# The two weight tiles of a block interleaved column by column in the weight buffers

## The chip, the cores and the metric

The kernel runs on one NeuronCore of a Trainium2 chip, as one launch. The metric is the device time in microseconds, the median of several executions. Three executions of the kernel before took 3079.48, 3080.9 and 3082.37 us. A fourth one was profiled, and all rows below come from that one.

## The reference

Two transformer-like blocks run one after the other on 256 tokens of width 2048, in float32. The first has a mixer (a gated delta rule and a gated convolution), cross attention on 256 memory tokens and a squared-ReLU MLP. The second has latent attention, neighbourhood attention, a Fourier mix and a gated convolutional feed-forward net, with a modulation worked out from one conditioning vector. What fills the time is the chain of dense products between them, of which these lines are typical:

```python
h = h + hybrid_mixer(rms_norm(h, norm_mix_g[i]), w_in[i], ...)          # x @ w_in, ... @ w_out
h = h + memory_cross_attention(rms_norm(h, norm_xa_g[i]), rms_norm(mem, norm_mem_g[i]), ...)
h = h + squared_relu_mlp(rms_norm(h, norm_mlp_g[i]), mlp_w1[i], mlp_w2[i])
...
x = x + gt1 * (jnp.concatenate([o_mla, o_na, o_fn], axis=-1) @ w_out[l])
x = x + gt2 * conv_ffn(h2, w_up[l], conv_w[l], conv_b[l], w_down[l])
```

## The kernel before

All dense weights are laid out on the host in one array `stream` of slots. A slot is 128 partitions x 1024 float32 columns, 512 KB, and there are 906 of them. A `Phase` is one dense product: `nblocks` blocks of `ncol` output features (256, in the two `kr` phases 128), each block made of `chunks` chunks of 128 input features. A slot holds `per_slot` chunks of one block (4; in `kr` 8), chunk after chunk, each `ncol` columns wide.

SyncE's queue loads the slots in order into a ring of eight buffers `raw`. ScalarE rounds each slot into one of four `whi` buffers (L823, fp32r, the reduced float32 that TensorE takes in one pass), and VectorE writes the remainder `raw - whi` into the matching `wlo` buffer (L1218). The activations are split in the same way into `act[:, 0]` and `act[:, 1]` (or `hid`). One product is then three matmuls: high weights with high activations, high with low, low with high.

TensorE's loop is `phase` (L448 is its matmul). For each block it waits for a free PSUM bank, for each slot for `split_done`, and then runs over the chunks of the slot, over the two halves `hf` of the block's 256 output features and over the three matmuls. In an ordinary phase the 128 x 128 weight tile is the stationary operand `lhs` and the 128 x 256 activations are the moving operand `rhs`; the two halves write the two halves of one PSUM bank. In a flipped phase (`memv`, `nav_c`, `nav_x`, `v_c`, `v_x`) the activations are the stationary operand and all 256 weight columns of the chunk the moving one. After the last matmul of a slot `slot_used` tells ScalarE that the `whi` and `wlo` buffers may be written again; it waits for nothing finer than a slot.

In the weight buffers of an ordinary phase a chunk's 256 columns stand in the order of the output features: first the 128 columns of half 0, then the 128 of half 1. Every weight tile is thus read with step one. The order of the work is written out: the phases follow each other in one fixed list, and each engine has its own copy of that order.

The modulation is worked out beside phases marked `mod`: VectorE accumulates `modacc` (L1204, L1423), and TensorE sums it in short matmuls with a one-column moving operand (L463, function `mod_matmuls`). Other short float32 matmuls are row sums (L469), a norm's spreading over partitions (L473), and those of the delta rule (L586 to L643). L586 and L588 take a stationary operand whose 128 columns are one column repeated.

Of the kernel before, what the change touches and what calls it, by code (L numbers as in the profile page):

```python
# [14 lines left out]
P = 128  # L15
# [112 lines left out]
def build(nc, x_t, mem_t, ctx_t, stream, mods, pvec, eye, cmix, catt, na_bias, na_mask, out_t):  # L128
    es = ExitStack()
    with es:  # L130
# [288 lines left out]
        def _(pe):  # L419
            c = Counts(pe)  # L420

            def phase(ph, src, c0=0, after=None):

                def body(i):
                    for k in range(ph.K):
                        b = bank[(ph.block0 + k) % 2]

                        pe.wait_ge(block_free, i * ph.K + (ph.block0 + k + 1))  # L430
                        for sl in range(ph.slots_per_block):
                            j = k * ph.slots_per_block + sl

                            pe.wait_ge(split_done, i * ph.S + (ph.slot0 + j + 1 + RAW_N))
                            if after and k == 0:
                                c.at(after[0], after[1] + (sl + 1) * after[2])
                            buf = (ph.slot0 + j) % SPL_N
                            for ci in range(ph.per_slot):
                                kc = sl * ph.per_slot + ci
                                for hf in range(ph.ncol // P if not ph.flip else TT):  # L440
                                    for n, (wx, ax) in enumerate(((whi, 0), (whi, 1), (wlo, 0))):
                                        if ph.flip:
                                            lhs = src[:, ax, c0 + kc, hf * P:(hf + 1) * P]
                                            rhs = wx[:, buf, ci * NCOL:(ci + 1) * NCOL]
                                        else:
                                            lhs = wx[:, buf, ci * ph.ncol + hf * P:ci * ph.ncol + (hf + 1) * P]
                                            rhs = src[:, ax, c0 + kc, :]
                                        mm = pe.matmul(b[:, hf * T:(hf + 1) * T], lhs, rhs,  # L448
                                                       start=(kc == 0 and hf == 0 and n == 0),
                                                       stop=(kc == ph.chunks - 1 and n == 2), skip_group_check=True)  # L450
                            mm.then_inc(slot_used, 1)
                            if ph.mod and j == MOD_OUT_AT:
                                mod_matmuls(ph, i)
                for i in range(ph.iters):
                    body(i)

            def mod_matmuls(ph, i):

                mb = i + ph.mod0
                pe.wait_ge(mod_used, mb * 8 + (8 + MOD_N))  # L460
                for w in range(ph.mod):
                    for n in range(MOD_COL // P):
                        mm = pe.matmul(bank[2][:, 4 * w + n:4 * w + n + 1], modacc[:, w, n * P:(n + 1) * P],  # L463
                                       ones[:, 0:1], start=True, stop=True, skip_group_check=True)
                mm.then_inc(mod_out, 1)
# [1267 lines left out]
def slots_of(w, ph, cols=None):  # L1733


    if cols is not None:
        w = np.concatenate([w[:, a:b] for a, b in cols], axis=1)
    n = ph.nblocks * ph.ncol
    assert w.shape == (ph.chunks * P, n), (ph.name, w.shape)
    w = w.reshape(ph.slots_per_block, ph.per_slot, P, ph.nblocks, ph.ncol)  # L1740
    return w.transpose(3, 0, 2, 1, 4).reshape(ph.slots, P, SLOT)


# [127 lines left out]
```

## Time and profile before

| what | value |
|---|---|
| median of three executions | 3080.9 us (3079.48 to 3082.37) |
| the profiled execution | 3077.71 us |
| its span, first to last instruction | 3075.9 us |
| what lies around the span | 1.8 us |
| mean granted TensorE clock | 0.970 |
| TensorE matmul / weight load busy | 2901.8 us / 2838.5 us |
| VectorE / ScalarE busy | 2096.0 us / 1331.7 us |
| weight slots loaded | 906 of 512 KB |

PE is TensorE's matmuls, PEld its weight loads, DVE VectorE, ACT ScalarE. A group is written out<-in; for L448 the two names behind the arrow are the moving and the stationary operand, so `bank<-act,whi` is an ordinary phase and `bank<-whi,act` a flipped one. Float32 operands that aren't fp32r show two records for each matmul. Busy matmul time is a modelled length and not a rate: matmuls overlap in the pipeline. The rate is read from the distance between starts, or from the number of records in a stretch.

### The profile page before, as it was taken

What the parts mean: (1) busy time and instruction counts of PE and PEld (TensorE: products, weight loads), DVE (VectorE), ACT (ScalarE), POOL (GpSimd) and SP (SyncE); (2) the same over time, 40 slices, a digit from 0 to 9 for tenths busy, and PEclk for the clock granted to TensorE, in tenths of its full rate; (3) what the DMA queues carried; (4) which work ended last, traced back from release to release, by engine and by line L of the source; (5) the groups of instructions that cost most, each with busy time, mean ns of one, the idle gap of its engine ahead of it and who ended that gap; (6) DMA issues with size and microseconds to landing.
All of it is one profiled execution on the core that took longest, in us unless ns stands there. A gap on an engine that the chain in (4) does not pass through costs nothing.

```text
span 3075.9 us, 55206 instructions
## 1 busy us (share of the span) xinstructions
PE 2901.8 (94%) x23858; PEld 2838.5 (92%) x23858; DVE 2096.0 (68%) x2934; ACT 1331.7 (43%) x1646; POOL 5.1 (0%) x13
## 2 busy tenths in 40 slices
PE   7998888999999899999999989988998999999998
PEld 7998787999998899999999979967598999999998
DVE  6988654698977877676766775454457665665665
ACT  4445323443433453444435444434345543554453
POOL 0000000000000000000000000000000000000000
PEclk9999898999999999999999989998999999999999
DMA  5554102577664677777777745522144565555553
GB/s 203 188 169 165 55 1 80 204 254 260 245 227 168 240 289 275 280 274 268 287 268 267 282 140 178 190 98 96 55 156 153 195 199 196 191 195 196 192 195 117
DMA packets 160451, 591.58 MB, mean 192 GB/s; under 512 B 17840, under 2 KB 17840, under 8 KB 159696
## 3 DMA queue, kind: packets, MB, share of 16 engines
q1 hardware_dynamic: 159264, 579.93, 53.4%
q0 software_dynamic: 944, 8.12, 0.7%
q8 instruction: 188, 3.08, 0.4%
q14 instruction: 55, 0.45, 0.1%
HBM read 585.88 MB, written 2.10 MB: 191 GB/s over the span
## 4 chain that ended last, share of the span: by engine, by line
PE 86%; DVE 10%; ACT 2%; issue 1%; DMA 1%; SPq 0%; DVEq 0%; ACTq 0%
PE bank L448 76%; DVE wlo L1218 2%; PE bank L712 1%; DVE ev L1237 1%; DVE modacc L1423 1%; PE bank L469 1%; PE bank L463 1%; PE bank L616 1%; PE bank L473 1%; DVE tmp L1373 1%; PE bank L614 1%; PE bank L608 1%; DVE ev L1340 1%; PE bank L687 1%; ACT whi L823 1%
## 5 line engine op out<-in xcount | busy, mean ns | idle before, releaser
L448 PE MATMUL bank<-act,whi 128*128 128x256 f32 x10144 | 1784.4, 281 | 59.7 <-DVE wlo L1218 20.2
L448 PEld LDWEIGHTS bank<-act,whi 128*128 128x128 f32 x10144 | 1560.0, 191 | 65.4 <-issue 34.1
L1218 DVE TENSOR_TENSOR wlo<-raw,whi 128x1024 fp32r<-128x1024 f32 x906 | 1098.1, 1223 | 530.2 <-ACT whi L823 528.4
L448 PE MATMUL bank<-act,wlo 128*128 128x256 f32 x5072 | 1421.7, 280 | 0.0
L823 ACT ACTIVATE whi<-raw 128x1024 fp32r<-128x1024 f32 x906 | 948.2, 1057 | 898.0 <-PE bank L448 897.4
L448 PEld LDWEIGHTS bank<-act,wlo 128*128 128x128 f32 x5072 | 969.4, 191 | 0.0
L448 PE MATMUL bank<-hid,whi 128*128 128x256 f32 x3456 | 602.5, 279 | 0.0
L448 PEld LDWEIGHTS bank<-hid,whi 128*128 128x128 f32 x3456 | 524.5, 188 | 0.0
L448 PE MATMUL bank<-hid,wlo 128*128 128x256 f32 x1728 | 482.1, 279 | 0.0
L1204 DVE SCALAR_TENSOR_TENSOR modacc<-modraw,small,modacc 128x512 f32<-128x512 f32 x480 | 348.6, 747 | 11.0 <-DMA modraw<-mods 5.6
L448 PEld LDWEIGHTS bank<-hid,wlo 128*128 128x128 f32 x1728 | 328.8, 190 | 0.0
L448 PE MATMUL bank<-whi,act 128*128 128x256 f32 x896 | 158.1, 279 | 0.0
L448 PEld LDWEIGHTS bank<-whi,act 128*128 128x128 f32 x896 | 136.5, 188 | 0.0
L448 PE MATMUL bank<-wlo,act 128*128 128x256 f32 x448 | 125.0, 279 | 0.0
L1293 DVE SCALAR_TENSOR_TENSOR ev<-bank,pv,ev 128x255 f32<-128x255 f32 x176 | 76.9, 478 | 62.8 <-ACT ev L888 61.3
L1423 DVE SCALAR_TENSOR_TENSOR modacc<-modraw,modacc 128x256 f32<-128x256 f32 x232 | 98.6, 481 | 0.1
L448 PEld LDWEIGHTS bank<-wlo,act 128*128 128x128 f32 x448 | 84.1, 188 | 0.0
L888 ACT ACTIVATE ev<-bank,pv 128x256 f32<-128x256 f32 x88 | 45.0, 561 | 70.4 <-PE bank L448 70.4
L901 ACT ACTIVATE ev<-h 128x512 f32<-128x512 f32 x40 | 25.3, 632 | 113.6 <-DVE h L1268 68.0
L1282 DVE TENSOR_TENSOR hid<-ev,hid 128x512 fp32r<-128x512 f32 x32 | 22.2, 693 | 72.8 <-ACT hid L877 72.8
L893 ACT ACTIVATE ev<-ev 128x256 f32<-128x256 f32 x44 | 18.4, 419 | 80.1 <-DVE ev L1293 80.1
L1014 ACT ACTIVATE tmp<-bank 128x512 f32<-128x512 f32 x28 | 16.7, 597 | 73.6 <-PE bank L608 73.6
(269 smaller groups left out, 1545.3 us busy)
## 6 DMA issues: line engine op xcount, KB each, us to landing
raw<-stream SPq DMA_DIRECT2D x906, 512.0 KB, 4.4
modraw<-mods SPq DMA_DIRECT2D x192, 512.0 KB, 4.1
h<-x_t SPq DMA_DIRECT2D x4, 512.0 KB, 6.3
memV<-mem_t POOLq DMA_DIRECT2D x1, 2048.0 KB, 8.6
tmp<-ctx_t POOLq DMA_DIRECT2D x1, 2048.0 KB, 12.5
out_t<-tmp SPq DMA_DIRECT2D x4, 512.0 KB, 2.6
cz<-catt POOLq DMA_DIRECT2D x1, 1216.0 KB, 12.2
bias<-na_bias POOLq DMA_DIRECT2D x1, 1024.0 KB, 5.1
```

The lines of the kernel that those rows point to most:

```text
L448: mm = pe.matmul(b[:, hf * T:(hf + 1) * T], lhs, rhs, start=(kc == 0 and hf == 0 and n == 0), stop=(kc == ph.chunks - 1 and n == 2), skip_ ...
L463: mm = pe.matmul(bank[2][:, 4 * w + n:4 * w + n + 1], modacc[:, w, n * P:(n + 1) * P], ones[:, 0:1], start=True, stop=True, skip_group_che ...
L469: return pe.matmul(out, src[:, tok], ones[:, 0:1], start=start, stop=stop, skip_group_check=True)
L473: return pe.matmul(out, small[:, col + n:col + n + 1].to_broadcast([P, P]), ident[:, :], start=start, stop=True, skip_group_check=True)
L608: mm = pe.matmul(bk(hg, 0)[:, n, :], MT[hg][:, n, :], X[hg][:, n, :], start=True, stop=True)
L614: pe.matmul(bk(hg, 2)[:, n, :], XT[hg][:, n, :], Y[hg][:, n, :], start=True, stop=True)
L823: sc.activation(whi[:, at % SPL_N, :], raw[:, at % RAW_N, :], ACT.Copy).then_inc(hi_done, 1)
L888: ins = sc.activation(ev[:, 0, hf * T:(hf + 1) * T], b2(b)[:, hf, :], ACT.Identity, scale=par("ff_conv", n * 6 + (6 * first + 3 * hf + 1)) ...
L1204: ins = ve.scalar_tensor_tensor(acc, wt, col, acc, ALU.mult, ALU.add)
L1218: ve.tensor_tensor(wlo[:, at % SPL_N, :], raw[:, at % RAW_N, :], whi[:, at % SPL_N, :].bitcast(F32), ALU.subtract).then_inc(split_done, 1)
L1293: ins = ve.scalar_tensor_tensor(o, b2(b)[:, hf, so], par("ff_conv", n * 6 + (6 * first + 3 * hf + j)), o, ALU.mult, ALU.add)
L1423: ins = ve.scalar_tensor_tensor(acc, x_, w, acc, ALU.mult, ALU.add)
```

## The change

The host lays the 256 columns of a chunk in another order, for ordinary phases only: column 0 of half 0, column 0 of half 1, column 1 of half 0, column 1 of half 1, and so on. The kernel's `lhs` for half `hf` is then every second column, starting at column `hf`: a stationary operand of 128 columns with a step of two elements (8 bytes) where it had one of a step of one (4 bytes). The splits on ScalarE and VectorE work on whole slots, whatever the order of their columns. Flipped phases keep their layout and operands. In the `kr` phases, where a block has 128 columns, the expression gives the same operand as before. No buffer moves, and no instruction, wait or transfer is added or taken away.

```diff
@@ phase, TensorE
                                         else:
-                                            lhs = wx[:, buf, ci * ph.ncol + hf * P:ci * ph.ncol + (hf + 1) * P]
+                                            cols = wx[:, buf, ci * ph.ncol:(ci + 1) * ph.ncol]
+                                            lhs = cols.rearrange("p (n a) -> p a n", a=ph.ncol // P)[:, hf, :]
                                             rhs = src[:, ax, c0 + kc, :]
@@ slots_of, on the host
     w = w.reshape(ph.slots_per_block, ph.per_slot, P, ph.nblocks, ph.ncol)
+    if not ph.flip:
+        w = w.reshape(w.shape[:-1] + (ph.ncol // P, P)).swapaxes(-1, -2).reshape(w.shape)
     return w.transpose(3, 0, 2, 1, 4).reshape(ph.slots, P, SLOT)
```

## Rows read from the trace of the kernel before

**Rows 1.** The page: span, busy time and share of each engine, instructions

```profile
span 3075.9 us, 55206 instructions
PE 2901.8 (94%) x23858; PEld 2838.5 (92%) x23858; DVE 2096.0 (68%) x2934; ACT 1331.7 (43%) x1646; POOL 5.1 (0%) x13
```

**Rows 2.** The page: chain that ended last, share of the span by engine

```profile
PE 86%; DVE 10%; ACT 2%; issue 1%; DMA 1%; SPq 0%; DVEq 0%; ACTq 0%
```

**Rows 3.** Windows: stretch, busy and records of each engine, clock, DMA share, GB/s

```profile
1300.00:1500.00 200.00, 200.00 (x1702) 200.00 (x1701) 140.89 (x162) 90.02 (x97) 0.00 (x0) 1.00 0.75 277
...
2400.00:2600.00 200.00, 200.00 (x1767) 200.00 (x1766) 126.94 (x170) 93.24 (x109) 0.00 (x0) 1.00 0.58 193
```

**Rows 4.** The page: groups, busy us, mean ns, idle before and its releaser

```profile
L448 PE MATMUL bank<-act,whi 128*128 128x256 f32 x10144 | 1784.4, 281 | 59.7 <-DVE wlo L1218 20.2
...
L1218 DVE TENSOR_TENSOR wlo<-raw,whi 128x1024 fp32r<-128x1024 f32 x906 | 1098.1, 1223 | 530.2 <-ACT whi L823 528.4
L448 PE MATMUL bank<-act,wlo 128*128 128x256 f32 x5072 | 1421.7, 280 | 0.0
L823 ACT ACTIVATE whi<-raw 128x1024 fp32r<-128x1024 f32 x906 | 948.2, 1057 | 898.0 <-PE bank L448 897.4
...
L448 PE MATMUL bank<-hid,whi 128*128 128x256 f32 x3456 | 602.5, 279 | 0.0
...
L448 PE MATMUL bank<-hid,wlo 128*128 128x256 f32 x1728 | 482.1, 279 | 0.0
...
L448 PE MATMUL bank<-whi,act 128*128 128x256 f32 x896 | 158.1, 279 | 0.0
...
L448 PE MATMUL bank<-wlo,act 128*128 128x256 f32 x448 | 125.0, 279 | 0.0
```

**Rows 5.** Waits: who waited for whom, us in total, times, longest

```profile
ACT whi L823 <- PE bank L448: 897.4, 568, 8.5
...
DVE wlo L1218 <- ACT whi L823: 528.4, 433, 6.9
```

**Rows 6.** Timeline, weight loads at 2500 us: start us, us, instruction, count

```profile
2499.97 0.19 PEld L448 LDWEIGHTS bank<-act,wlo 128*128 128x128 f32 x1
...
2500.99 0.19 PEld L448 LDWEIGHTS bank<-act,wlo 128*128 128x128 f32 x1
```

**Rows 7.** Timeline, weight loads at 1500 us

```profile
1500.03 0.19 PEld L448 LDWEIGHTS bank<-act,wlo 128*128 128x128 f32 x1
...
1501.09 0.19 PEld L448 LDWEIGHTS bank<-act,wlo 128*128 128x128 f32 x1
```

**Rows 8.** Chain in order of time: start us, us, what, count

```profile
655.31 45.33 PE bank L448 x384
...
1735.70 45.34 PE bank L448 x384
...
2341.11 719.92 PE bank L448 x6336
```

**Rows 9.** Timeline, weight loads of L463 (one moving column) and after them

```profile
653.36 1.87 PEld L463 LDWEIGHTS bank<-ones,modacc 128*128 128x128 f32 x16
655.14 0.30 PEld L448 LDWEIGHTS bank<-act,whi 128*128 128x128 f32 x2
```

**Rows 10.** Timeline, weight loads of the delta rule at 424 to 429 us

```profile
424.54 0.47 PEld L591 LDWEIGHTS bank<-ident,qkvT 128*128 128x128 f32 x4
...
425.41 0.97 PEld L586 LDWEIGHTS bank<-cz,gt 128*128 128x128 f32 x8
...
428.07 0.97 PEld L598 LDWEIGHTS bank<-tmp,qkvT 128*128 128x128 f32 x8
```

**Rows 11.** Timeline of weight loads from 490 us

```profile
490.54 6.51 PEld L469 LDWEIGHTS bank<-ones,tmp 128*128 128x128 f32 x32 [2.02 <-ACT tmp L1031]
```

**Rows 12.** Window inside that stretch, columns as in rows 3

```profile
491.00:495.00 4.00, 4.00 (x21) 4.00 (x20) 0.00 (x0) 1.72 (x2) 0.00 (x0) 0.50 0.00 0
```

## The prediction before the run

> **What bounds the kernel now.** I read the page first: of a span of 3075.9 us TensorE's matmuls are busy for 94% and its weight loads for 92%, VectorE for 68% and ScalarE for 43% [rows 1]. The chain that ended last runs over PE for 86% [rows 2]. The windows say why a busy share isn't enough here: in 200 us inside the MLP and in 200 us inside the feed-forward net both matmuls and loads are busy all the time at full clock, and yet the first holds 1701 loads and the second 1766 [rows 3]. So the thing to read is the pace, the distance from one weight load to the next.
>
> The waits show which way the work leans. ScalarE's split waits 897.4 us for TensorE to give a buffer back, and VectorE's split waits 528.4 us for ScalarE [rows 5]; TensorE waits for VectorE's split for only 20.2 us in its largest group [rows 4]. TensorE is the bound, and everything else of the weight path is cover.
>
> Now the pace itself. At 2500 us nine loads take 2500.99 - 2499.97 = 1.02 us, 113.3 ns each [rows 6]. At 1500 us nine take 1501.09 - 1500.03 = 1.06 us, 117.8 ns each [rows 7]. Both are the same instructions with the same shapes, at a granted clock of 1.00 [rows 3]. The chain in order of time shows that each pace holds for long: nineteen pieces of 384 matmuls at 45.33 or 45.34 us (118 ns) between 655 and 1781 us, and 6336 in 719.92 us (113.6 ns) at the end [rows 8]. I call them the long and the short pace.
>
> What sets them? The moving operand is 256 columns; if it takes one column in each cycle of 2.4 GHz, that is an estimated 106.7 ns. The weight load can be seen nearly alone where the moving operand has one column: sixteen loads from 653.36 to 655.14 us, 111.3 ns each [rows 9]. By that estimate load and matmul are almost equally long. At half the clock 32 such loads take 6.51 us, or (6.51 - 0.33)/31 = 199 ns each if the last one lasts 0.33 us [rows 11, 12]: the pace goes with TensorE's clock, so it isn't a fixed time for issue. A load of the main loop has at most 113.3 - 111.3 = 2 ns of cover at the short pace and 6.5 ns at the long one. That is why this change can matter at all.
>
> **The change part by part.** *Host layout.* No device time. *Transfers and splits.* The slots are as large as before, and L823 and L1218 read and write them whole; their 1057 and 1223 ns [rows 4] stay. If they did not, they have the waits of rows 5 as cover. *Flipped phases*, 896 + 448 matmuls [rows 4]: untouched. *The two `kr` phases*, one block of 16 chunks and 3 matmuls each, 96 in all: same operand. *Ordinary phases*: 10144 + 5072 + 3456 + 1728 - 96 = 20304 loads [rows 4] read their 128 columns over 1024 bytes of each partition instead of 512. This is the only term: 20304 x d, where d is what a load's step adds to the pace. 1 ns of d is 20.3 us, 0.66% of the time. Nothing is re-ordered, so no wait and no queue moves; `slot_used` still comes after both halves of a slot.
>
> No load in the trace has a step of two, so d has to be bounded.
>
> *From below.* The nearest rows are loads at the other end, with all 128 columns taken from one address. L586 in rows 10 has eight such loads in 0.97 us, (0.97 - 0.19)/7 = 111 ns each; L598, eight loads of adjacent columns, gives the same 0.97 us. How many bytes the columns are spread over doesn't show there, from 4 to 512. The transposes of L591 give (0.47 - 0.14)/3 = 110 ns, though each of their loads is recorded at about 0.14 us instead of 0.19 [rows 10, 6]: so float32 columns can be fetched faster than the main loop's loads fetch them, by some 50 ns in 128 columns, and what holds an ordinary load to 107 to 111 ns is then probably not the reading of adjacent bytes. That speaks for d = 0. A gain isn't excluded: the short pace is 113.3 against 110 to 111 in rows 9 and 10, and if the two streams of reads hinder each other, another order of addresses may free them. The bound is 2.3 ns for the short-paced loads and 6.5 ns for the long-paced ones.
>
> *From above.* If a load's 107 ns were set by the bytes that it passes over, twice the bytes would take 213 ns, and with the 4.6 ns that lie between 106.7 and 111.3 the pace would be 218 ns: d = 104.7 and 100.2 ns at the two paces, about 102.6 ns on average.
>
> I take d = 0, since one address against 512 bytes made no difference, and keep both ends.
>
> The Trainium skill has a rule that speaks against the change: "SBUF — State Buffer", section "Door 1: The DMA port swizzle", says that SBUF is read in lines of 16 bytes, that each crossing to a new line costs, and that at least two hits in a line are needed to hide this. Step two in float32 crosses twice as often, 64 lines a load and not 32, but has exactly two hits in each; so by the letter of the rule d is still 0, on its very edge. No row here has a step between one address and the next line, so the trace neither confirms nor denies it.
>
> The sum: 3077.7 us of the profiled execution (3075.9 of span and 1.8 around it) + 20304 x 0 = 3077.7 us. The median of the three runs lies 3.2 us higher, so on that scale it is 3080.9 us.
>
> **The rivals.**
>
> *The paces change hands, faster.* The long pace isn't a matter of addresses in the source: the same loop has both. Of the 21744 matmuls of L448 the nineteen pieces hold 7296, and with the shorter pieces beside them I estimate 10,000 long-paced ones and 11,000 short-paced ones. The first long-paced piece of rows 8 begins right behind the one-column matmuls of rows 9; my guess is that load stream and matmul stream can lock in two ways, and that such a break picks one. A load that reads other addresses may tip the lock. All at the short pace: 10,000 x 4.5 ns = 45 us less, 3036 us. Against it: three runs within 2.9 us say that the locks fall in the same way each time, and equal load times should leave them so.
>
> *The paces change hands, slower.* The same, with the short pace lost: 11,000 x 4.5 = 49.5 us more, 3130 us. Both streams would now walk at the same speed, 1024 bytes in 107 ns, where they walked at two different ones; a conflict, once there, would last for the whole matmul.
>
> *A price for each new line.* The mechanism of this kernel: 32 more lines in each of 20304 loads, with 2 ns of cover. With one cycle for each (0.417 ns at 2.4 GHz) a load grows by 13.3 ns; less the 2 or 6.5 ns of cover, some 9 ns remain, 180 us more, 3264 us. It decides where the short-paced loads alone grow by 6 us/10,300 = 0.6 ns past their cover, at (2 + 0.6)/32 = 0.08 ns a line. Where the skill's SBUF page says "each access that crosses to a new line pays a penalty", this is what it would be.
>
> *The load is bound by bytes passed over.* d = 102.6 ns: 20304 x 102.6 = 2083 us more, 5164 us. For it: a load is at the limit now. Against it: rows 10. Nothing else would become late; ScalarE and VectorE would only wait longer for TensorE.
>
> **How the numbers follow.** No change of pace: 0.60, with a range of its own of 3075 to 3087 us. Locks to the short pace: 0.10. A freer load that passes even the short pace (down to 111 ns everywhere, 3080.9 - 45 - 49 = 2987 us): 0.02. Locks to the long pace: 0.10. A price for each line: 0.10. Bound by bytes: 0.08. To leave out no more than 2 in 10 the range reaches over both lock rivals, 3034 to 3135 us: 0.60 + 0.10 + 0.10 = 0.80. Within 0.2% (6 us, about what a measurement of this kernel can tell from no change) 0.60, faster 0.12, slower 0.28.
>
> **What the profile after would show.** Right: 1701 and 1766 loads in the windows of rows 3, a pace of 113.3 and 117.8 ns at the places of rows 6 and 7, and the same waits as rows 5. Lock: the same two paces, but pieces of 384 in 43.5 us, or of 6336 in 746. A price for a line: one new pace over 118 ns in ordinary phases, with flipped phases still at 113 to 118, and the wait of L823 for TensorE grown by about as much as the span. Bytes: PEld records longer than 0.19 us and a pace near 218 ns. The prediction is wrong if the load's fetch has no spare rate at step two, which only the transposes' shorter load lets me hope for.

## The result, and the profile after

The change makes the kernel slower: 3160.18 us (3158.47 to 3161.47, four runs) against 3080.19 us (3073.06 to 3082.37, four runs) on the same chip, a ratio of 1.0263 with a 95% interval of 1.0246 to 1.0281. The time lies above the stated range, which ended at 3135 us.

The page after. TensorE is still the bound; both its shares rise a little, and the instructions are the same in number. The line numbers behind L448 have moved by one.

```profile
span 3156.7 us, 55206 instructions
PE 2990.5 (95%) x23858; PEld 2927.9 (93%) x23858; DVE 2102.5 (67%) x2934; ACT 1332.4 (42%) x1646; POOL 5.1 (0%) x13
PE 87%; DVE 9%; ACT 2%; issue 1%; DMA 1%; SPq 0%; DVEq 0%; ACTq 0%
L449 PE MATMUL bank<-act,whi 128*128 128x256 f32 x10144 | 1854.2, 284 | 53.6 <-DVE act L1368 14.4
L1219 DVE TENSOR_TENSOR wlo<-raw,whi 128x1024 fp32r<-128x1024 f32 x906 | 1101.8, 1222 | 586.8 <-ACT whi L824 580.4
L824 ACT ACTIVATE whi<-raw 128x1024 fp32r<-128x1024 f32 x906 | 948.9, 1057 | 965.8 <-PE bank L449 963.5
```

The splits cost what they did [rows 4], 1057 and 1222 ns. ScalarE waits 963.5 us for TensorE instead of 897.4 [rows 5], 66 us more while the span grew by 81: it stands farther behind the bound, as it would behind a TensorE that has become slower by itself.

The same two windows as in rows 3, and the weight loads at the place of rows 6, of the changed kernel:

```profile
1300.00:1500.00 200.00, 200.00 (x1671) 200.00 (x1670) 138.18 (x158) 88.27 (x96) 0.00 (x0) 1.00 0.73 271
2400.00:2600.00 200.00, 200.00 (x1669) 200.00 (x1668) 127.77 (x179) 91.48 (x114) 0.00 (x0) 1.00 0.58 187
```

```profile
2499.87 0.19 PEld L449 LDWEIGHTS bank<-act,wlo 128*128 128x128 f32 x1
...
2500.95 0.19 PEld L449 LDWEIGHTS bank<-act,wlo 128*128 128x128 f32 x1
```

Before, the two windows held 1701 and 1766 loads; now they hold 1670 and 1668. Nine loads take 2500.95 - 2499.87 = 1.08 us, 120.0 ns each. The two paces of 113.3 and 117.8 ns have become one in the ordinary phases, above both. The chain in order of time shows where that leaves the microseconds; each piece has its counterpart in rows 8:

```profile
1105.29 46.20 PE bank L449 x384
...
2378.95 762.49 PE bank L449 x6336
```

The last stretch of 6336 matmuls went from 719.92 to 762.49 us, 42.6 us of the 80.8 us by which the span grew. The nineteen pieces of 384 went from 45.34 to 46.20 us; one of them, in the flipped phase `memv`, stayed at 45.34, so the other 18 give 15.5 us. The rest is spread over the other pieces. Over 20304 changed loads the growth is 4.0 ns each.

### The profile page after: what moved, and what is told of

Its sections match the earlier page's. It is cut to its first block, busy times and chain, and to the rows that moved or that the text cites. A ratio compares the mean times of both kernels' runs of the same rounds, so it can differ in the third digit from the quotient of the medians.

```text
span 3156.7 us, 55206 instructions
## 1 busy us (share of the span) xinstructions
PE 2990.5 (95%) x23858; PEld 2927.9 (93%) x23858; DVE 2102.5 (67%) x2934; ACT 1332.4 (42%) x1646; POOL 5.1 (0%) x13
## 4 chain that ended last, share of the span: by engine, by line
PE 87%; DVE 9%; ACT 2%; issue 1%; DMA 1%; SPq 0%; DVEq 0%; ACTq 0%
PE bank L449 77%; DVE wlo L1219 2%; PE bank L713 1%; DVE ev L1238 1%; DVE modacc L1424 1%; PE bank L470 1%; PE bank L464 1%; PE bank L617 1%; DVE tmp L1374 1%; PE bank L474 1%; PE bank L615 1%; PE bank L609 1%; DVE ev L1341 1%; PE bank L688 1%; ACT whi L824 1%
## 5 line engine op out<-in xcount | busy, mean ns | idle before, releaser
L449 PE MATMUL bank<-act,whi 128*128 128x256 f32 x10144 | 1854.2, 284 | 53.6 <-DVE act L1368 14.4
L449 PEld LDWEIGHTS bank<-act,whi 128*128 128x128 f32 x10144 | 1616.4, 196 | 58.6 <-issue 33.4
L1219 DVE TENSOR_TENSOR wlo<-raw,whi 128x1024 fp32r<-128x1024 f32 x906 | 1101.8, 1222 | 586.8 <-ACT whi L824 580.4
L449 PE MATMUL bank<-act,wlo 128*128 128x256 f32 x5072 | 1442.6, 284 | 0.0
L824 ACT ACTIVATE whi<-raw 128x1024 fp32r<-128x1024 f32 x906 | 948.9, 1057 | 965.8 <-PE bank L449 963.5
L449 PEld LDWEIGHTS bank<-act,wlo 128*128 128x128 f32 x5072 | 993.7, 196 | 0.0
L449 PE MATMUL bank<-hid,whi 128*128 128x256 f32 x3456 | 623.5, 282 | 0.0
L449 PEld LDWEIGHTS bank<-hid,whi 128*128 128x128 f32 x3456 | 545.1, 194 | 0.0
L449 PE MATMUL bank<-hid,wlo 128*128 128x256 f32 x1728 | 488.5, 283 | 0.0
L609 PE MATMUL bank<-tmp 128*128 128x128 f32 x224 | 33.4, 299 | 15.5 <-DVE tmp L1526 8.6
```

The lines of the kernel that those rows point to most:

```text
L449: mm = pe.matmul(b[:, hf * T:(hf + 1) * T], lhs, rhs, start=(kc == 0 and hf == 0 and n == 0), stop=(kc == ph.chunks - 1 and n == 2), skip_ ...
L609: mm = pe.matmul(bk(hg, 0)[:, n, :], MT[hg][:, n, :], X[hg][:, n, :], start=True, stop=True)
L824: sc.activation(whi[:, at % SPL_N, :], raw[:, at % RAW_N, :], ACT.Copy).then_inc(hi_done, 1)
L1219: ve.tensor_tensor(wlo[:, at % SPL_N, :], raw[:, at % RAW_N, :], whi[:, at % SPL_N, :].bitcast(F32), ALU.subtract).then_inc(split_done, 1)
```

## The experiments

The question is why a weight load that takes every second column lengthens the pace by 2 to 7 ns. I name the candidates by what a load of 128 columns touches: with step one 512 bytes, 32 lines of 16 bytes; with step two 1024 bytes, 64 lines. The kernels from step four to the one with a moving step of two were run once each, so no interval stands beside their times; the readings rest on the distances between their loads.

**Step four**, an interleave of four tiles instead of two, with the host layout to match:

```diff
-                                            lhs = wx[:, buf, ci * ph.ncol + hf * P:ci * ph.ncol + (hf + 1) * P]
+                                            if ph.ncol == NCOL:
+                                                tile, a = ci * 2 + hf, 4
+                                                cols = wx[:, buf, tile // a * a * P:(tile // a + 1) * a * P]
+                                                lhs = cols.rearrange("p (n a) -> p a n", a=a)[:, tile % a, :]
...
+        w = w.reshape(ph.slots, P, 8 // 4, 4, P).swapaxes(-1, -2).reshape(ph.slots, P, SLOT)
```

> Four weight tiles (two chunks, two halves) interleaved, so that each weight load of an ordinary phase has a step of four elements, 16 bytes; the result is the same. After the change the pace of ordinary phases was 120.0 ns a matmul at full clock, against 113.3 or 117.7 before. Theory 1 (a price for each 16-byte line that a load enters): a load enters 128 lines where it entered 64, and with one hit in each. The growth from 32 to 64 lines was 6.7 ns against the shorter pace, so 64 more lines cost at least 13.4 ns more: a pace of 133 ns or above, near 3430 us. Theory 2 (the extra comes from the step not being one, whatever its size): 120 ns again, 3160 us. Theory 3 (load and moving operand collide when they walk through their bytes at the same speed, 1024 bytes in the length of one matmul): at step four they walk at different speeds again, so the pace falls back below 120 ns.

It took 5449.23 us. The loads of this kernel in the timeline:

```profile
2466.53 0.33 PEld L453 LDWEIGHTS bank<-act,wlo 128*128 128x128 f32 x1
...
2470.03 0.33 PEld L453 LDWEIGHTS bank<-act,wlo 128*128 128x128 f32 x1
```

Fifteen loads in 3.50 us, 233.3 ns each. The pace nearly doubled with the step. Theory 2 (any step but one costs the same) and theory 3 (the two streams collide only when they walk equally fast) fall; theory 1 had the direction, but where it asked for at least 13.4 ns more, 113 ns were added. The same kernel a little earlier, with its window:

```profile
2456.03 0.33 PEld L453 LDWEIGHTS bank<-act,wlo 128*128 128x128 f32 x1
...
2458.83 0.33 PEld L453 LDWEIGHTS bank<-act,wlo 128*128 128x128 f32 x1
```

```profile
2456.00:2459.00 3.00, 3.00 (x14) 3.00 (x14) 2.25 (x3) 0.00 (x0) 0.00 (x0) 0.50 0.15 42
```

Here the granted clock was 0.50 (1.2 GHz), and twelve loads took 2.80 us, again 233.3 ns. This length doesn't go with TensorE's clock, unlike that of a load with adjacent columns [rows 11, 12].

**Step zero**, all columns of a load from one address (the other columns are left out):

```diff
-                                            lhs = wx[:, buf, ci * ph.ncol + hf * P:ci * ph.ncol + (hf + 1) * P]
+                                            at = ci * ph.ncol + hf * P
+                                            lhs = wx[:, buf, at:at + 1].to_broadcast([P, P])
```

> The kernel before, but in ordinary phases all 128 columns of a weight load are the first column of the tile, repeated (step zero), so that a load stays in one 16-byte line; this leaves out the other columns, the products are other numbers. Theory 1 (price for each line): 31 lines fewer than before take away up to 6.5 ns, and the pace falls to the moving operand's own, 107 to 111 ns; near 2960 us. Theory 2 (adjacent bytes are the fast path, anything else pays): 120 ns, 3160 us. Theory 3 (collision of the two streams): something other than 113.3 and 117.7, most likely 107 to 111 ns.

It took 3068.28 us, against a single run of 3074.59 us of the kernel before on that chip. Its windows, pieces of its chain, and loads from the first of these pieces:

```profile
1300.00:1500.00 200.00, 200.00 (x1718) 200.00 (x1717) 141.93 (x164) 90.12 (x98) 0.00 (x0) 1.00 0.75 272
2400.00:2600.00 200.00, 200.00 (x1767) 200.00 (x1766) 126.40 (x167) 90.83 (x105) 0.00 (x0) 1.00 0.59 195
```

```profile
1083.69 46.19 PE bank L449 x384
1130.66 43.64 PE bank L449 x384
1175.09 44.91 PE bank L449 x384
...
2331.49 720.12 PE bank L449 x6336
```

```profile
1083.88 0.31 PEld L449 LDWEIGHTS bank<-act,whi 128*128 128x128 f32 x2
...
1085.56 0.19 PEld L449 LDWEIGHTS bank<-act,wlo 128*128 128x128 f32 x1
```

Loads from one line gained next to nothing, so the expectation of 2960 us was wrong, and so was a price that simply adds up by the line. The run doesn't give the length of such a load, though: the moving operand was as before, and it turns out below that this operand holds the pace. The pieces show more. Beside one-line loads the same matmuls ran at 43.64 us/384 = 113.6 ns, at 44.91/384 = 117.0 ns and at 46.19/384 = 120.3 ns; in the last of these fourteen loads take 1085.56 - 1083.88 = 1.68 us, 120.0 ns each. That is the pace of the changed kernel, without a step of two.

**Half of the moving columns**, with step one and with step two (the products of the other tokens are left out in 94 of 96 matmuls of a block):

```diff
+                                        w_ = T if (kc == 0 and n == 0) or ph.flip else T // 2
+                                        rhs = rhs[:, 0:w_]
-                                        mm = pe.matmul(b[:, hf * T:(hf + 1) * T], lhs, rhs,
+                                        mm = pe.matmul(b[:, hf * T:hf * T + w_], lhs, rhs,
```

> The kernel before, but in ordinary phases only 128 of the 256 moving columns are streamed in 94 of 96 matmuls of a block; this leaves out half of the tokens' products. Weight loads are unchanged, with step one. It shows the load without a full-length matmul over it. Load is what sets the pace: 111 to 113 ns a matmul stays, near 3030 us. Load and matmul only bind together: the pace falls clearly below 107 ns, as far as the load's own length.

> The changed kernel with the same cut to 128 moving columns. Theory 1 (lines) and any theory by which the step-two load is itself longer: the pace stays at 120 ns, some 7 to 9 ns above the same cut with step one. Theory 3 (collision with the moving operand): with the moving operand busy for half of the time the extra is halved or gone, so both cuts lie within 3 ns of each other.

They took 4887.06 and 4896.52 us: with half as many moving columns in each matmul the mean granted clock fell to 0.621 and 0.622, and the expected 3030 us was missed for that reason. Both hold the same 470 loads in a window at clock 0.50, 213 ns each, but they differ in a stretch of such matmuls at 1.00, which both have right behind a flipped phase, whose matmuls keep their 256 columns. First the kernel with step one, then that with step two:

```profile
3150.00:3190.00 40.00, 40.00 (x360) 40.00 (x360) 18.15 (x15) 17.81 (x19) 0.00 (x0) 1.00 0.58 195
2500.00:2600.00 100.00, 100.00 (x471) 100.00 (x470) 39.60 (x45) 21.82 (x22) 0.00 (x0) 0.50 0.45 158
```

```profile
3150.00:3190.00 40.00, 40.00 (x342) 40.00 (x342) 17.58 (x15) 16.77 (x18) 0.00 (x0) 1.00 0.55 184
2500.00:2600.00 100.00, 100.00 (x471) 100.00 (x470) 38.93 (x44) 21.82 (x22) 0.00 (x0) 0.50 0.45 158
```

40 us / 360 = 111.1 ns and 40 us / 342 = 117.0 ns. The load sets the pace even beside a matmul of half the length, and step two lengthens it by 6 ns there. At half the clock step two is free: the pace of 213 ns is longer than the 117 ns that the load with step two took in the other window.

**Step three and step eight.** The first reads every third column from a stretch of 384 (columns of other tiles; the products are other numbers), the second interleaves all eight tiles of a slot.

```diff
+                                                at = (ci + hf) * P
+                                                cols = wx[:, buf, at:at + 3 * P]
+                                                lhs = cols.rearrange("p (n a) -> p a n", a=3)[:, 0, :]
```

```diff
+                                                tile, a = ci * 2 + hf, 8
```

> The kernel before with a step of three elements (12 bytes) in the weight loads of ordinary phases; it reads columns that belong to other tiles of the same slot, so the products are other numbers. So far: step two, 64 lines of 16 bytes a load, 120.0 ns; step four, 128 lines, 233 to 236 ns. Theory A (each line that a load enters takes a fixed time, 120/64 = 1.88 or 235/128 = 1.84 ns, and the load takes the longer of that and its own length): 96 lines, 176 to 180 ns a matmul, near 4270 us. Theory B (two hits in a line hide it, fewer don't, as the rule of the lines reads by its letter): a third of the lines has two hits and the others one; a threshold would put the load near 235 ns, as step four, near 5450 us.

> All eight weight tiles of a slot interleaved: a step of eight elements, 32 bytes, same result. A load then enters 128 lines, as at step four, but passes over 4096 bytes instead of 2048. Theory A (lines entered): 233 to 236 ns as at step four, 5449 us within some 3%. Theory C (bytes passed over, which fits steps two and four as well: 120 and 235 ns for 1024 and 2048 bytes): about 470 ns, near 10,000 us.

Step three took 4211.54 us, step eight 5576.63 us. Their loads in the timeline:

```profile
2409.76 0.26 PEld L453 LDWEIGHTS bank<-hid,wlo 128*128 128x128 f32 x1
...
2411.84 0.26 PEld L453 LDWEIGHTS bank<-hid,wlo 128*128 128x128 f32 x1
```

```profile
1999.69 0.34 PEld L453 LDWEIGHTS bank<-hid,wlo 128*128 128x128 f32 x1
...
2001.86 0.34 PEld L453 LDWEIGHTS bank<-hid,wlo 128*128 128x128 f32 x1
```

Twelve loads in 2.08 us are 173.3 ns, nine in 2.17 us are 241 ns. By bytes passed over (theory C) step eight would have doubled step four; it is within 4% of it, so bytes are out and lines remain. The 4% between two loads of 128 lines each is not explained. By a threshold of two hits (theory B) step three would have been like step four; it lies at 96 lines x 1.81 ns.

**The moving operand.** Its 256 columns are 64 lines too. Two kernels repeat one moving column (the other tokens are left out), with loads of step one and of step two; a third gives the moving operand a step of two across a pair of chunks (other products), with loads of step one.

```diff
-                                            rhs = src[:, ax, c0 + kc, :]
+                                            rhs = src[:, ax, c0 + kc, 0:1].to_broadcast([P, T])
```

```diff
-                                            rhs = src[:, ax, c0 + kc, :]
+                                            pair = src[:, ax, c0 + kc - kc % 2:c0 + kc - kc % 2 + 2, :]
+                                            rhs = pair.rearrange("p k (t a) -> p (k t) a", a=2)[:, :, kc % 2]
```

> The kernel before, but in ordinary phases the 256 moving columns are all the chunk's first column, repeated, so that the moving operand stays in one 16-byte line where it entered 64; this leaves out all other tokens. Loads have step one. Theory M (the moving operand's lines are under the same limit of 1.8 to 1.9 ns each: 64 x 1.77 = 113.3, 64 x 1.84 = 117.7, and that makes the two paces): both paces go, and what is left is the load's own 111 to 112 ns, near 3000 us. Rival (the two paces have nothing to do with lines of the moving operand): 113.3 and 117.7 ns stay, 3070 to 3107 us.

> The changed kernel (loads with step two) with the same moving operand of one repeated column. Theory A (the load's own 64 lines take 120 ns): 120.0 ns, 3160 us, and 8 ns above the same kernel with step one. Theory 3 (the load is only longer because the moving operand reads beside it): with the moving operand in one line the pace falls to that of step one, 111 to 113 ns.

> The kernel before, but the moving operand of ordinary phases has a step of two elements (every second column of a pair of chunks; other products). It then enters 128 lines. If the limit on lines holds for the moving operand too: 128 x 1.82 to 1.88 = 233 to 240 ns a matmul, near 5450 us. If it holds for weight loads alone: 113 to 120 ns, near 3100 us.

They took 3003.13, 3110.78 and 5358.84 us. A window of each, in this order:

```profile
2600.00:2700.00 100.00, 100.00 (x898) 100.00 (x897) 69.68 (x104) 50.14 (x66) 0.00 (x0) 1.00 0.61 201
```

```profile
2600.00:2700.00 100.00, 100.00 (x852) 100.00 (x851) 62.00 (x84) 44.26 (x54) 0.00 (x0) 1.00 0.57 188
```

```profile
2600.00:2650.00 50.00, 50.00 (x219) 45.34 (x219) 18.28 (x20) 9.52 (x9) 0.00 (x0) 1.00 0.43 157
```

With one moving line the load of step one runs at 100/897 = 111.5 ns, its own length as in rows 9 (111.3 ns), and in the ordinary phases both paces of the kernel before are gone: it was the reading of 256 adjacent moving columns that lifted 111.5 to 113.3 or 117.8. The load of step two keeps 100/851 = 117.5 ns; that is its own, without help from the moving operand. It was expected at 120.0 ns and 3160 us, so 2.5 ns of the changed kernel's pace and 49 us of its time are missing here: they come only with an adjacent moving operand. With the moving operand at 128 lines the matmul takes 50/219 = 228 ns, a little less than the expected 233 to 240. A line costs both readers about the same where the line count is high.

The last stretch of 6336 matmuls splits the change's cost there. It took 719.92 us before [rows 8] and 762.49 us after; loads of step two beside one moving column took

```profile
2345.61 747.91 PE bank L449 x6336
```

Of the 42.6 us the load's own length thus makes 28.0, and the other 14.6 come only beside the adjacent moving operand. In a piece of 384 between 1091 and 1782 us this kernel took 45.33 us, as the kernel before did: there the load's own 117.5 ns were covered, and the whole growth to 46.20 us is of the second kind.

**The two paces.** What decides between them was tried by one more small matmul behind each of the modulation's groups, in the kernel before:

```diff
                 mm.then_inc(mod_out, 1)
+                for _ in range(1):
+                    pe.matmul(bank[7][:, 0:128], act[:, 0, 0, 0:P], act[:, 0, 0, 0:128], start=True, stop=True,
+                              skip_group_check=True)
```

and the same with 2 columns.

> The kernel before with one more fp32r matmul (128 moving columns, into an unused bank) behind each group of one-column matmuls of the modulation, 24 in all. It asks what makes the two paces of the kernel before. Theory L (how the load stream and the matmul stream happen to start after a break decides which of two paces holds until the next break): the pieces between 655 and 1781 us may change from 117.7 to 113.3 ns a matmul, some 30 us less for 7296 matmuls. Rival (the pace belongs to the place, for instance to the traffic of the modulation's transfers): 117.7 ns stays, and the time is within 5 us of the kernel before.

> As the kernel with 128 moving columns more, but with 2. Theory L: the start after the break is another one again, so the paces of the pieces may come out in either way, but only as 113.3 or 117.7 ns. Rival: 117.7 ns stays.

> The kernel before with one two-column matmul more behind each group of the modulation's matmuls, now timed against the kernel before. In its profile 13,300 of the 21,300 counted matmuls had the shorter pace. Theory L: the kernel before comes out at either of two times, near 3075 and near 3105 us, as the long last stretch takes the one or the other pace, and so does this kernel, near 3070 and 3098 us; the ratio's interval takes in 1. Rival: a steady gain of 0.3%.

The first two were run once each and took 3096.67 and 3069.99 us. One run of the kernel before on that chip took 3106.56 us, which is the higher of the two times that it has, as will be seen. The chain of the kernel with 128 columns, then of that with 2:

```profile
974.83 43.59 PE bank L448 x384
1079.22 45.28 PE bank L448 x384
...
2331.50 748.08 PE bank L448 x6336
```

```profile
1087.64 43.65 PE bank L448 x384
...
1359.98 43.65 PE bank L448 x384
1404.53 45.34 PE bank L448 x384
1450.76 43.65 PE bank L448 x384
...
2332.73 721.08 PE bank L448 x6336
```

A later run of the kernel with two columns, on another chip, took 3092.28 us and left this chain:

```profile
1083.41 45.34 PE bank L448 x384
...
1355.75 45.34 PE bank L448 x384
1401.98 43.65 PE bank L448 x384
...
2326.60 749.00 PE bank L448 x6336
```

In these kernels a piece of 384 takes 43.6 or 45.3 us, nothing between; in the kernel with two columns more the two alternate from piece to piece between 1087 and 1766 us. The same program took 721.08 us for its last stretch in one run and 749.00 us in another, and these two runs lie 22 us apart. In the same place, the first such piece behind 1080 us, it had 43.65 us in the one run and 45.34 us in the other. So the rival, a pace that belongs to the place, falls, and so does one that the program alone fixes: the paces change at breaks between stretches and last from one to the next, as theory L has it. What in a break picks the pace is not shown. The 128 columns moved only three of the nineteen pieces to the short pace and left the fifteen between 1079 and 1772 us at 45.28, so most of the 30 us that were thought possible there did not come; its longer last stretch may be the same chance as in the other kernels. The kernel before fits in: its 17 runs on the last chip lie at 3071.71 to 3082.69 us (13) and at 3105.06 to 3114.03 us (4), about as far apart as the 28 us between 721.08 and 749.00; no profile of a run in the upper group was kept. The kernel with two columns more has 8 of 12 runs at 3063.51 to 3071.47 us and 4 at 3092.28 to 3097.65 us. Its ratio is 0.9964, with an interval of 0.9926 to 1.0002: no gain that this can tell.

## Why the prediction was wrong

The step that failed is the choice of d. "I take d = 0, since one address against 512 bytes made no difference": that row was true, but it lies wholly on the side where the load's own 107 to 111 ns cover the fetch. It says nothing about where the cover ends. In place of 0 the runs showed 4.0 ns a load on average, 6.7 ns at the short pace and 2.2 ns at the long one. The runs put these lengths side by side:

| load, moving operand | lines of each | pace at full clock | ns a line of the longer |
|---|---|---|---|
| step zero, adjacent | 1, 64 | 113.6, 117.0 or 120.3 ns | (load's own length not seen) |
| step one, one column repeated | 32, 1 | 111.5 ns | (load's own length) |
| step one, adjacent | 32, 64 | 113.3 or 117.8 ns | 1.77, 1.84 |
| step two, one column repeated | 64, 1 | 117.5 ns | 1.84 |
| step two, adjacent (the change) | 64, 64 | 120.0 ns | 1.88 |
| step three, adjacent | 96, 64 | 173.3 ns | 1.81 |
| step four, adjacent | 128, 64 | 233.3 ns | 1.82 |
| step eight, adjacent | 128, 64 | 241 ns | 1.88 |
| step one, step two | 32, 128 | 228 ns | 1.78 |

From 96 lines on the runs fit one 16-byte line in 1.8 to 1.9 ns, and at step four this didn't follow TensorE's clock. By this account a load takes the longer of its own 111.5 ns and its lines. At step one the lines take an estimated 32 x 1.84 = 59 ns and hide; at step two 64 x 1.84 = 118 ns, just past the cover, where 117.5 ns were measured. This overhang of 6.0 ns in the load by itself is one part of the cost: the kernel with step two and one moving column took 3110.78 us, about 30 us above the kernel before. The other part, about 50 us from there to 3160.18 us, is the step from 117.5 to 120.0 ns beside the adjacent moving operand. Its cause is open. The count of lines doesn't fix it: with 64 moving lines and one-line loads the pace was 113.6, 117.0 or 120.3 ns.

Point by point. *What bounds the kernel*: right; TensorE's load was the shortest lever, and nothing else moved. *Cover of 2 and 6.5 ns*: right, as the step-one load alone has 111.5 ns. A load that grows by 6.0 ns would then cost 4 ns at the short pace and nothing at the long one; 6.7 and 2.2 ns were measured, and the 2.5 ns or so on top of both are the open part. *The transposes' shorter load as a sign of spare fetch*: wrong inference. By the estimate above there was spare rate at step one, nearly a factor of two, but step two needed slightly more than that factor. The prediction's last sentence named this as its weak point. *Untouched parts* (flipped phases, splits, transfers): right; the piece in `memv` stayed at 45.34 us. *The lock rivals*: paces that hold from break to break do exist, but the change did not move loads from one of the two to the other; it put one pace above both. As step zero has this third pace too, in some pieces, a lock may have a share in the open part. *A price for each new line*: the right mechanism at 0.10, named with a price of 0.417 ns beyond a fixed load, which gave 3264 us. The price is 1.8 to 1.9 ns, four times that, but it replaces the load's length instead of adding to it, and so the load by itself grew by 6.0 ns and not by 13.3. This rival's picture of the profile, one new pace over 118 ns in the ordinary phases and the flipped one as before, is what the page shows. *Bytes passed over*: shown wrong by step eight.

One warning was already in the prediction's rows: 64 moving lines in 113.3 or 117.8 ns where matmuls with one moving column took 111. I read this excess as a lock of two streams alone. It goes away with the moving operand's spread (111.5 ns with one column repeated), so it was also a sign that 64 lines are near a limit.

The skill's rule of the lines (Trainium skill, "SBUF — State Buffer", "Door 1: The DMA port swizzle") names the right unit. Its condition, two hits in a line to hide the access, is not what the runs show: with two hits a line the load by itself took 117.5 ns instead of 111.5 at full clock, and at half the clock both steps had 213 ns. The measurement decides: here the hits that are needed are those that bring the lines' time below the engine's own.

Open: why step two beside an adjacent moving operand takes 120.0 ns when each of the two alone stays at or below 117.8, why one-line loads beside it take 120.0 ns in some pieces, and what in a break picks the pace. No run here settles any of the three.

## What to carry to other kernels

An operand's step is not free or dear by itself: count the 16-byte lines that it enters, take as an estimate from these runs 1.8 to 1.9 ns for each, and compare this with what the engine needs anyway at its clock. By that estimate the float32 weights of this kernel have nearly half of the time to spare at step one and none at step two; beyond it the load's length grew with the lines, 173.3 ns for 96 and 233.3 ns for 128, and hardly further at step eight. Where the count comes out level with the engine's own time, as here, expect a few ns that it doesn't give. If a trace shows two stable rates for the same instructions, do not call a cost in that place zero before one of the two operands has been taken out of the way.

## What the runs showed of the hardware

- Weight load and moving operand come out at nearly the same price, 1.8 to 1.9 ns for each 16-byte line: 233.3 ns for 128 lines in a load, 228 ns for 128 in a moving operand. In step four it was 233.3 ns at a granted clock of 0.50 and of 1.00.
- 128 moving columns a matmul instead of 256 brought the mean granted clock from 0.970 to 0.621, with TensorE's matmuls recorded as busy for 97% of the span; the kernel took 4887.06 us for half of the moving work.
- The kernel before has two times, 3072 to 3083 us and 3105 to 3114 us in 17 runs. With one small matmul more behind each group of the modulation, one and the same program had 6336 matmuls of the last stretch at 113.8 ns in one run and at 118.2 ns in another.
- Beside weight loads from one address, matmuls with 256 adjacent moving columns ran at 113.6, 117.0 and 120.3 ns in different pieces of one run, at a granted clock of 1.00.
